# Routing of a mixture-of-experts layer taken tile by tile, with the first gather ahead of the block list

## The reference

```python
xp = xp + merge_heads(y_ssm, o, att_norm_g[l], w_out[l])
xp = xp + moe_ffn(rms_norm(xp, norm_ffn_g[l]), w_router[l], b_router[l], ...)

def moe_ffn(h, ...):
    logits = (xt @ w_router + b_router).astype(jnp.float32)
    top_val, top_idx = lax.top_k(logits, TOP_K)
    gates = jax.nn.softmax(top_val, axis=-1)
    ...                       # tokens sorted by expert, in blocks
    gu = xb @ w_gate_up[e] + b_gate_up[e]
    gate = jnp.minimum(gu[:, :D_FF], SWIGLU_LIMIT)
    up = jnp.clip(gu[:, D_FF:], -SWIGLU_LIMIT, SWIGLU_LIMIT)
    act = (up + 1) * gate * jax.nn.sigmoid(gate * SWIGLU_ALPHA)
    return act @ w_down[e] + b_down[e]
```

## Time and profile before

| | us |
|---|---|
| median of three runs | 1373.37 |
| lowest, highest | 1373.23, 1373.82 |
| the profiled execution, its own time | 1375.36 |
| its span, first to last instruction | 1373.6 |
| PE busy | 1285.4 (94%) |
| DVE busy | 492.7 (36%) |
| ACT busy | 254.1 (18%) |
| POOL busy | 34.6 (3%) |

### The profile page before, as it was taken

One profiled execution on the slowest core, in us unless ns is written; L12 is line 12 of the kernel. 1 busy time (PEld: TensorE's weight loads), 2 busy tenths in 40 slices (PEclk: granted clock), 3 DMA queues, 4 the chain that ended last, 5 costly groups with the idle time before them and its releaser, 6 DMA issues.

```text
span 1373.6 us, 17176 instructions
## 1 busy us (share of the span) xinstructions
PE 1285.4 (94%) x6469; PEld 553.5 (40%) x6470; DVE 492.7 (36%) x960; ACT 254.1 (18%) x446; POOL 34.6 (3%) x58
## 2 busy tenths in 40 slices
PE   6999997994899999999999999999999999999995
PEld 4665753553333333333333333333333333333332
DVE  2533444543423332333334233332333332333334
ACT  1031224442111111111111111111111111111112
POOL 2000002003000000000000000000000000000000
PEclk9999997995899999999999999999999999999998
DMA  9422135033599953996899999999999997999994
GB/s 327 180 87 98 62 123 161 9 123 123 223 411 428 419 233 134 396 429 274 326 430 428 428 429 429 428 428 428 428 428 429 429 392 287 430 428 428 428 429 173
DMA packets 43400, 436.31 MB, mean 318 GB/s; under 512 B 5717, under 2 KB 6861, under 8 KB 18806
## 3 DMA queue, kind: packets, MB, share of 16 engines
q1 hardware_dynamic: 38288, 428.36, 74.9%
q0 software_dynamic: 2080, 6.48, 1.5%
q10 hardware_dynamic: 3014, 1.23, 0.4%
HBM read 432.33 MB, written 3.72 MB: 317 GB/s over the span
## 4 chain that ended last, share of the span: by engine, by line
PE 70%; DMA 24%; DVE 2%; ACT 1%; POOL 1%; issue 1%; ACTq 0%; SPq 0%; DVEq 0%; POOLq 0%
PE PS L1655 27%; DMA ring<-in_w_gate_up_dram 23%; PE PS L1690 12%; PE PS L1186 7%; PE PS L1195 5%; PE PS L1622 4%; PE PS L1595 4%; PE PS L1148 3%; PE PS L1197 1%; PE PS L1478 1%; DMA ring<-in_w_in_dram 1%; PE PS L1644 1%; PE PS L1337 1%; PE PS L1323 1%; PE PS L1428 1%
## 5 line engine op out<-in xcount | busy, mean ns | idle before, releaser
L1655 PE MATMUL PS<-ring,r 128*64 128x512 f32 x2304 | 527.4, 598 | 22.3 <-DMA ring<-in_w_gate_up_dram 21.1
L1655 PEld LDWEIGHTS PS<-ring,r 128*64 128x64 f32 x2304 | 156.0, 137 | 318.8 <-issue 269.7
L1690 PE MATMUL PS<-ring,r 128*64 128x512 f32 x1152 | 255.2, 595 | 0.2
L1087 DVE SCALAR_TENSOR_TENSOR r<-PS,gprev,r 128x512 f32<-128x512 f32 (+1 forms) x222 | 155.9, 742 | 223.4 <-PE PS L1622 223.4
L1690 PEld LDWEIGHTS PS<-ring,r 128*64 128x64 f32 x1152 | 82.2, 137 | 148.3 <-issue 148.3
L1127 DVE TENSOR_TENSOR yy<-PS,yy 128x512 fp32r<-128x512 f32 x36 | 24.9, 691 | 253.3 <-ACT yy L692 253.3
L683 ACT ACTIVATE r<-r 128x512 f32<-128x512 f32 x36 | 22.7, 629 | 493.2 <-DVE r L1113 493.2
L1148 PE MATMUL PS<-ident,r 128*128 128x128 f32 (+5 forms) x490 | 82.9, 299 | 21.1 <-DMA gffn<-in_norm_ffn_g_dram 11.0
L1186 PE MATMUL PS<-r,ring 128*128 128x323 f32 x320 | 90.6, 441 | 0.6 <-DMA ring<-in_w_in_dram 0.6
L1622 PE MATMUL PS<-yy,place 64*128 64x512 f32 x444 | 82.4, 449 | 4.5 <-DVE r L1087 3.0
L1148 PEld LDWEIGHTS PS<-ident,r 128*128 128x128 f32 (+5 forms) x490 | 62.6, 185 | 47.3 <-issue 19.9
(11 more groups left out here) (277 smaller groups left out, 784.3 us busy)
## 6 DMA issues: line engine op xcount, KB each, us to landing
ring<-in_w_gate_up_dram SPq DMA_DIRECT2D x128, 2048.0 KB, 18.1
ring<-in_w_down_dram SPq DMA_DIRECT2D x64, 2048.0 KB, 17.8
ring<-in_w_in_dram SPq DMA_DIRECT2D x8, 2048.0 KB, 18.5
ring<-in_w_out_dram SPq DMA_DIRECT2D x3, 2048.0 KB, 7.7
r<-in_x_prompt_dram SPq DMA_DIRECT2D x2, 512.0 KB, 4.2
r<-in_x_prompt_dram POOLq DMA_DIRECT2D x2, 512.0 KB, 3.5
r<-bias_table_clipped ACTq DMA_DIRECT2D x4, 256.0 KB, 7.0
out_dram<-r SPq DMA_DIRECT2D x2, 512.0 KB, 2.6
```

Source lines behind the costliest of these rows:

```text
L1087: v.scalar_tensor_tensor(xx, PS[0:rows, 6 + h, :], gprev[0:rows, t:t + 1], xx, ALU.mult, ALU.add)\
L1655: last = mm(PS[64 * h:64 * h + 64, m, :], xt[:, k % 4, k // 4, :], w[:, kk, D * m + 512 * h:D * m + 512 * h + 512], start=False, stop=(k = ...
L1690: last = mm(PS[64 * h:64 * h + 64, 2, :], at[:, kk, c, :], w[:, kk, 512 * h:512 * h + 512], start=(c == 0 and kk == 0), stop=(c == 1 and k ...
```

## The change

Output and arithmetic stay those of the reference. What it does:

- PE: turn_rows(0) and turn_attended(2) come ahead of att_part(3), the latter into bank 1. The third tile's attention output is turned unscaled; its norm factor is put in at the add (add_part: scalar_tensor_tensor in place of tensor_tensor for the tile's two attention parts), with a copy of the factor on the upper 64 partitions. DVE evicts the turned tile in one operation (it was ACT in four).
- Logits: a tile's eight products are made with the router's weights stationary, in four column tiles of 32, two products each (partial_logits). DVE copies the four partial sums to lgp, and one more matmul with stack (ones where the row and the column agree modulo 32) adds them and turns them.
- Order: normalised rows, top four and chosen come tile by tile. Positions come from two sets of matmuls. The exponential of the gates is waited for only behind the block list.
- Splits: ACT's high and middle parts are laid between the norms; the third tile is normalised on ACT in place of DVE; the first subtraction of the third tile goes from POOL to DVE, behind a wait for the second tile's last subtraction and ahead of the block list. The other five subtractions stay on POOL. The bias splits (both halves) go from DVE to POOL, ahead of the token splits.
- Block 0: one_hots(0) and selector(0) come ahead of the block list, gather(0) comes ahead of the list's transposes and ahead of PE's wait for route_ready and its register load, which now stand directly before the loop.

```diff
+        lgp = (view(r2, 1024, 128), view(r2, 1152, 128), view(r2, 1280, SS))
+        stack = sb("stack", [128, NE])
...
+            step(g.tensor_tensor(stack[:, :], row_of[:, :], ident[:, NE:2 * NE], ALU.add))
...
             pool.wait_ge(s["sout_out"], 2 * 16)
-            for t in range(NT):
+            for m in range(2):
+                raw, parts = b_gu[:, m, :], b_gu3[:, D * m:D * m + D]
+                pool.wait_ge(s["b_hi"], 2 * m + 1)
+                step(g.memset(parts[NE:2 * NE], 0.0))
+                for low in PART_ROWS[1:]:
+                    step(g.tensor_tensor(raw[low:128], raw[low:128], parts[low:128], ALU.subtract))
+                    last = g.tensor_copy(parts[low:128], raw[low:128])
...
+            for t in range(2):
+                pool.wait_ge(s["hi_ready"], t + 1)
                 if t:
                     pool.wait_ge(s["xb_ready"], t)
-                pool.wait_ge(s["xb_part"], 2 * t + 1)
-                g.tensor_tensor(xrest, xn[:, t, :], xb[t][:, 0, :], ALU.subtract).then_inc(s["xb_rest"], 1)
...
+                g.tensor_tensor(xrest, xn[:, t, :], xb[t][:, 0, :], ALU.subtract).then_inc(s["rest_ready"], 1)
+                pool.wait_ge(s["rest_ready"], t + 1)
+                pool.wait_ge(s["mid_ready"], t + 1)
                 g.tensor_tensor(xb[t][:, 2, :], xrest, xb[t][:, 1, :], ALU.subtract).then_inc(s["xb_ready"], 1)
+            pool.wait_ge(s["rest_ready"], 3)
+            pool.wait_ge(s["mid_ready"], 3)
+            g.tensor_tensor(xb[2][:, 2, :], xrest, xb[2][:, 1, :], ALU.subtract).then_inc(s["xb_ready"], 1)
...
             mean_square(0)
+            norm_att(2)
             half_turned(0)
-            attended_out(2)
+            high_parts(0)
             mean_square(1)
             half_turned(1)
+            middle_parts(0)
+            high_parts(1)
             mean_square(2)
-            half_turned(2)
-            for t in range(NT):
-                token_parts(t)
+            act.wait_ge(s["rstd2_ready"], 1)
+            a.activation(xn[0:SS, 2, :], x[0:SS, 2, :], ACT.Identity, scale=stat[0:SS, 8:9]).then_inc(s["xn_ready"], 1)
+            high_parts(2)
+            middle_parts(1)
+            middle_parts(2)
             act.wait_ge(s["rexp"], 1)
             a.activation(pv[:, :, :], pv[:, :, :], ACT.Exp).then_inc(s["pv_ready"], 1)
...
+            dve.wait_ge(s["att_mm"], 3)
+            v.tensor_tensor(mixA[:, :, TCOL[2]:TC], PS[:, 1, :].rearrange("p (k n) -> p k n", n=128)[:, :, 0:SS],
+                            bc(gout[:, 8:12].unsqueeze(2), 128, 4, SS), ALU.mult).then_inc(s["mixA_ready"], 1)
+            step(rstd(0))
+            normalised_rows(0)
             turned(0)
-            bias_parts(1)
+            dve.wait_ge(s["sqrt5"], 3)
+            step(v.reciprocal(stat[SS:128, 20:21], stat[0:SS, 20:21]))
+            step(v.reciprocal(stat[0:SS, 20:21], stat[0:SS, 20:21]))
+            add_att(3)
             step(v.memset(place[:, TC:128 * NT].bitcast(f32), 0.0))
-            route(0)
-            normalised_rows(0)
+            partial_logits(0)
             add_att(4)
+            logits_max(0)
+            top_four(0)
+            turned(1)
             add_att(5)
-            turned(1)
+            partial_logits(1)
+            step(rstd(1))
+            normalised_rows(1)
             turned(2)
-            route(1)
-            normalised_rows(1)
-            route(2)
-            normalised_rows(2)
+            logits_max(1)
+            partial_logits(2)
+            rstd(2).then_inc(s["rstd2_ready"], 1)
+            top_four(1)
+            dve.wait_ge(s["chosen_ready"], 2)
+            v.tensor_tensor(chosen01, chosen[:, 0, :], chosen[:, 1, :], ALU.add).then_inc(s["chosen01_ready"], 1)
+            dve.wait_ge(s["rstd2_ready"], 1)
+            logits_max(2)
+            top_four(2)
...
-            dve.wait_ge(s["pv_ready"], 1)
-            step(v.tensor_reduce(chosen[:, :, :], eq[:, :, :, :].rearrange("p t k e -> p t e k"), axis=X, op=ALU.add))
...
+            positions(0, 2, PS[:, 6, 0:2 * NE])
+            dve.wait_ge(s["pos_mm"], 2)
+            positions(2, 3, PS[:, 5, 0:NE])
...
+            one_hots(0, 0, 0)
+            selector(0)
+            dve.wait_ge(s["hi_ready"], 3)
+            dve.wait_ge(s["xb_ready"], 2)
+            v.tensor_tensor(xrest, xn[:, 2, :], xb[2][:, 0, :], ALU.subtract).then_inc(s["rest_ready"], 1)
+
+            count, nb, upto, t3 = PS[:, 2, 0:NE], nbk[:, 0, :], nbk[:, 1, :], nbk[:, 2, :]
...
             dve.sem_inc(s["o_ev"], 2)
+            gathered(0)
             total = dve.value_load(blocks[0:1, 0:1], min_val=NE, max_val=MAX_BLOCKS)
...
+            def partial_logits(t):
...
+                for j in range(2):
+                    for q in range(4):
+                        last = mm(PS[32 * q:32 * q + NE, lgt_bank(t), 0:ROWS[t]], wr[:, 2 * q + j, :], hfT[t][:, 2 * q + j, :],
+                                  start=(j == 0), stop=(j == 1))
+                last.then_inc(s["lgp_mm"], 1)
...
+                pe.wait_ge(s["pl_ready"], t + 1)
+                mm(PS[0:ROWS[t], lgt_bank(t), 256:256 + NE], lgp[t], stack[:, :], start=True, stop=True).then_inc(s["lgt_mm"], 1)
...
+            turn_rows(0)
+            turn_attended(2)
             att_part(3)
-            turn_rows(0)
+            partial_logits(0)
             pe.wait_ge(s["out_ev"], 13)
-            turn_attended(2)
+            att_part(4)
             logits(0)
             turn_rows(1)
-            att_part(4)
             att_part(5)
+            partial_logits(1)
+            turn_rows(2)
             logits(1)
-            turn_rows(2)
+            partial_logits(2)
...
-            pe.wait_ge(s["route_ready"], 1)
-            total = pe.value_load(blocks[0:1, 0:1], min_val=NE, max_val=MAX_BLOCKS)
             pe.wait_ge(s["xb_ready"], NT)
             gather(0)
+            pe.wait_ge(s["bej_ready"], 1)
+            for c in range(2):
+                last = tr(PS[0:1, 7, 128 * c:128 * c + 128], bej[:, c:c + 1])
+            last.then_inc(s["bej_mm"], 1)
+            turn(0)
+            places(0)
             pe.wait_ge(s["gates_ready"], 1)
...
-            turn(0)
-            places(0)
+            pe.wait_ge(s["brow_ready"], 2)
+            pe.wait_ge(s["route_ready"], 1)
+            total = pe.value_load(blocks[0:1, 0:1], min_val=NE, max_val=MAX_BLOCKS)
```

More of the change, by code:

```diff
@@ L858, in _ @@
             step(v.memset(xn[64:128, 2, :], 0.0))
[L860 to L867, removed]
+            step(v.memset(chosen[64:128, 2, :], 0.0))
             def softmax(i):
@@ L1003, in normalised_rows, with turned @@
                     .then_inc(s["xn_ready"], 1)
+            def turned(t):
+                rows = ROWS[t]
+                for h in range(2 if t == 2 else 1):
+                    dve.wait_ge(s["hf_mm"], 2 * t + h + 1)
+                    last = v.tensor_copy(hfT[t][:, 4 * h:4 * h + 4, :],
+                                         PS[:, hf_banks(t)[h], :].rearrange("p (k n) -> p k n", k=4)[:, :, 0:rows])
+                last.then_inc(s["hf_dve"], 1)
+            def partial_logits(t):
+                dve.wait_ge(s["lgp_mm"], t + 1)
+                v.tensor_copy(lgp[t], PS[:, lgt_bank(t), 0:ROWS[t]]).then_inc(s["pl_ready"], 1)
@@ new lines, in positions @@
+            def positions(t0, t1, found):
+                step(v.scalar_tensor_tensor(one[:, t0:t1, :], found.rearrange("p (t e) -> p t e", e=NE), 1.0,
+                                            chosen[:, t0:t1, :], ALU.add, ALU.mult))
+                step(v.tensor_scalar(pg[:, :, t0:t1].rearrange("p e t -> p t e"), one[:, t0:t1, :], -1.0, None, ALU.add))
+            dve.wait_ge(s["att_mm"], 3)
+            v.tensor_tensor(mixA[:, :, TCOL[2]:TC], PS[:, 1, :].rearrange("p (k n) -> p k n", n=128)[:, :, 0:SS],
+                            bc(gout[:, 8:12].unsqueeze(2), 128, 4, SS), ALU.mult).then_inc(s["mixA_ready"], 1)
@@ L1039, in _ @@
-            count, nb, upto, t3 = PS[:, 6, 96:128], nbk[:, 0, :], nbk[:, 1, :], nbk[:, 2, :]
-            step(v.memset(nbk[:, 3, :], 0.0))
-            step(v.tensor_scalar(nb, count, float(CAP), 1.0, ALU.is_gt, ALU.add))
-            for m in range(2, TC // CAP):
-                step(v.scalar_tensor_tensor(nb, count, float(CAP * m), nb, ALU.is_gt, ALU.add))
-            step(v.tensor_tensor_scan(upto, nb, nbk[:, 3, :], 0.0, ALU.add, ALU.add))
-            step(v.tensor_scalar(t3, upto, pidx[:, 0:1], None, ALU.is_le))
@@ L1091, in _ @@
             selector(0)
+            dve.wait_ge(s["hi_ready"], 3)
+            dve.wait_ge(s["xb_ready"], 2)
+            v.tensor_tensor(xrest, xn[:, 2, :], xb[2][:, 0, :], ALU.subtract).then_inc(s["rest_ready"], 1)
+            count, nb, upto, t3 = PS[:, 2, 0:NE], nbk[:, 0, :], nbk[:, 1, :], nbk[:, 2, :]
+            step(v.memset(nbk[:, 3, :], 0.0))
+            step(v.tensor_scalar(nb, count, float(CAP), 1.0, ALU.is_gt, ALU.add))
+            for m in range(2, TC // CAP):
```

(12 more changed lines are left out.)

163 lines of the change are left out of this document (74 added, 89 removed).

## The result

The changed kernel takes 1352.1 us (median, 1350.8 to 1354.5), the kernel before beside it 1373.3. The ratio is 0.985, with a 95% interval of 0.983 to 0.987. The forecast was 1353.8, with a range of 1349.8 to 1360.5.

What follows compares the result with a forecast made beforehand. Bound by PE: block 0's start passes to the end one to one. Stretch terms put block 0 at 334.4, corrections +0.3 and +0.9 at 335.6, gain 19.6: 1373.37 - 19.6 = 1353.8 us, range 1349.8 to 1360.5.

Steps and rivals of the forecast that it cites:

- To the last attention part: PE from 299.3: steps summing to 12.3 us, so the last attention part ends at 311.7, against 314.67 before.
- rival (b): Better: third tile's attention parts at full clock (3.6 us), register load hidden, no clock fall; gain beyond 22.9, chance 0.07.
- The partial logits: Router products in column tiles on PE: 0.6 us taken, between 0.46 from below and 1.94 from above.
- From there to the gather: After the last attention part, splits and routing run in parallel; splits end at 326.8, the main gain.
- DVE beside POOL: Correction for DVE and POOL slowing each other: two or three meetings on the path, +0.3 us.
- the routing strand on DVE: DVE's normalising, evictions, logits, top four, positions, one-hots and selector after the add at 312.6, ending at 322.2.
- the split strand: Norms and splits on DVE, ACT and POOL beside the routing; POOL's step ends at 322.0, before the third tile's subtraction.
- From the gather to block 0: Gather 4.05 us to 330.9, then list transposes, turn, places, gate transposes and register load 1.0; block 0 at 334.4.
- The fall of the clock in block 0: PE, half idle for 3.5 us before block 0, may fall to 1.2 GHz there; half of 1.75 us, +0.9.
- (a): Rival: small costs larger (column tiles not overlapping +2.7, two clock falls +3.5, contention +1); gain 10 to 16.5, chance 0.17.
- (c): Rival: block 0 moves, but the second expert's weights come no earlier and PE waits; 1372 to 1373 us, chance 0.04.
- (d): Rival: slower, bias split holds POOL, delaying token splits if both halves take over 47.8 us; chance 0.02.

Runs made afterwards that it cites:

- e5: Changed kernel without the two DVE steps subtracting one from the positions, the subtraction going into the copy to pcur; 1352.9 us, ratio to before 0.9838.
- e2: Changed kernel with both bias splits back on DVE, at their places in the kernel before; 1360.6 us, ratio to before 0.9899.
- e9: e7 with DVE copying expert_of and place_of ahead of gates4, and PE loading its register ahead of the gate transposes; 1349.1 us, ratio to before 0.9831.
- e7: e5 with a buffer of its own for the third tile's remainder, so DVE subtracts earlier, without waiting for xb_ready; 1351.1 us, ratio to before 0.9815.
- e1: Kernel before, with the wait for the exponential and the gate steps moved behind route_ready, one-hots and selector; 1365.0 us, ratio to before 0.9924.
- e10: Changed kernel with ACT scaling the third tile's attention output by its norm factor ahead of the turn, as before; 1355.2 us, ratio to before 0.9855.

## Why the prediction was right, step by step

Block 0 was forecast at 335.6 on the clock of the profile of before and came at 333.49; behind weigh_values(5) (at 297.2 in before) that is 38.4 against 36.5. The way is the one described: loads and blocks hang on one PE event, the shift passes through, the list runs beside the splits and the gather. Four terms were off, in both signs. The start of the gather was forecast at 29.6 behind weigh_values(5) and came at 29.48; that is luck, since the first two terms below were off by 1.75 and 1.6 us and cancelled.

- **To the last attention part** 14.5 us forecast, 12.75 measured. The two parts of the third tile took 1.95 and 1.95 instead of 4.99. In before they ran partly at the lower clock (granted 0.50 from 309 to 312); rival (b) had priced them at 3.6. The partial logits took 0.58, for a forecast of 0.6.
- **From there to the gather** 15.1 forecast, 16.7 measured. Here the step "DVE beside POOL" failed. The sum had two or three meetings at 0.1 us each. In fact one of them, L1039, cost 1.7 us on DVE; at most 1.47 of it lay on the path, for POOL was done with the buffer at 320.35 and DVE's subtraction began at 321.82. e5 could take back 0.7 of it, because POOL still held the next step. Two smaller meetings on the path, L1005 (0.95 for 0.75) and L1030 (0.48 for 0.17), add 0.5. I had a row for such a meeting and read it wrongly: the normalisation that took 1.04 in place of 0.75 was not slower. It started at 322.30, POOL's subtraction ended at 320.45 + 2.34 = 322.79, and 0.55 us later it was finished. The price is thus not a share of DVE's own duration, but what is left of POOL's, less 0.1 to 0.2 us (0.29 for 0.49 left here, 1.95 for 2.08 left in e2). Besides, the prediction's own terms for the routing strand on DVE add up to 321.2 and not to 322.2; with the split strand at 322.0 that moves its sum by 0.2 at most.
- **From the gather to block 0** 7.6 forecast, 7.05 measured. The gather took 3.69 for 4.05, and the register load is there in full: 1.19 us of "issue" before L1702, for a forecast of 1.0. e9, which loads the register earlier, has 0.46 left there by PE's timeline, where e7 has 1.93.
- **The fall of the clock in block 0**, +0.9 as half a chance, did not come in either profile of the changed kernel. It came in three experiments: the first 16 instructions of L1713 (L1717 in e2) take 3.6 us in the changed kernel, 4.87 in e2, 5.09 in e5 and 5.27 in e7. In e5 the granted clock is at 0.50 meanwhile, with a full clock before and after:

```profile
330.00:331.00 1.00, 0.22 (x2) 0.17 (x4) 0.68 (x2) 0.52 (x2) 0.00 (x0) 0.98 0.00 0
331.00:332.00 1.00, 1.00 (x6) 0.58 (x4) 0.30 (x1) 1.00 (x1) 0.58 (x1) 0.50 0.00 0
...
335.00:336.00 1.00, 1.00 (x8) 0.34 (x4) 0.00 (x0) 0.00 (x0) 0.00 (x0) 1.00 0.00 0
```

(The columns are the stretch, its length, busy time with count of PE, PEld, DVE, ACT and POOL, then the granted clock, DMA share and GB/s.) That is 1.5 us, near the 1.75 of the prediction. By its size it may be a part of the spread between runs of one kernel (up to 7 us here), but that is not shown: the profiled run of e5, which has the fall, is the shortest of its four.

Of the rivals, (a) did happen in one of its three costs, the contention, with more than the 1 us it was priced at, and was cancelled by (b)'s full-speed attention parts. (c) is refuted by the load 4.24 us behind block 0. (d), the bias splits on GpSimd: POOL's timeline of the changed kernel has its last step end at 270.9, 32 us before the token splits.

```profile
255.69 0.94 POOL L411 MEMSET b_gu<- 32x1024 bf16 x1
...
269.84 1.04 POOL L414 CAST b_gu<-r 32x1024 bf16<-32x1024 f32 x1
303.05 2.13 POOL L423 TENSOR_TENSOR r<-r 128x1024 f32<-128x1024 f32 x1 [32.18 <-ACT r L664]
```

They took 15.2 us; the bound was 21. And the advice of the Trainium skill against GpSimd, GPSIMD Engine Reference, section Engine selection, would have led wrong here: back on DVE, at their places of before, the biases cost 6.3 us.

## What to carry to other kernels

When the loop behind a stage is paced by events of its own, cost the stage alone and pass the shift on one to one. In the stage, look first for a wait that was put ahead of work that doesn't need it: one moved wait gave 9.2 of 21.5 us here. And cost a DVE step beside a GpSimd step by what is left of the GpSimd step, not by its own length, unless a trace shows that its form is not held: a step of 0.2 us can take 2.

## What the runs showed of the hardware

Most DVE steps that read SBUF alone ended only when the running GpSimd step had ended, and were not merely slowed: a 128x64 subtraction took 1.95 where its 128x32 piece took 0.20, its form with two inputs 1.99, and a 64x1024 subtraction 3.17 in place of 1.22. A reduction from SBUF and a step from PSUM were not held (0.19), nor, in the changed kernel, the inversion of one column (0.16 at 314.71, beside a POOL step from 313.39 to 315.51), nor e1's one-input step over 128x96 (0.33). What sets the last one apart no run here shows. In the other direction a GpSimd step that began together with a DVE subtraction took 3.20 in place of 2.12 (e7). The Trainium skill, GPSIMD Engine Reference, section Key points, says that GpSimd shares its SBUF interfaces with VectorE, in contention with instructions in a 2-port performance mode or with two SBUF inputs. The two steps with two inputs agree with that. Which of the others ran in such a mode the profile doesn't tell. The section gives no length; here the wait lasted to the end of the other engine's step.

In two profiles the clock fell from 2.4 to 1.2 GHz right behind a short wait of PE. In e10 PE had waited 1.51 us until 301.43; the granted clock was 0.50 from 302 to 305, and att_part(3) took 5.27 for 3.70. In e5 it had waited 1.00 us until 330.78; the clock was 0.50 from 331 to 334, and block 0's first weights took 5.09. But in the changed kernel, behind a wait of 1.34 us ahead of block 0, the clock stayed at 1.00. So the length of the last wait alone doesn't decide it; what does, these runs don't show.
